# Twenty high parts of weight units made by ScalarE instead of GpSimd, around the two output projections of block 1 and the input of block 2's first layer

## The reference, cut to what matters

```python
x = layer_norm(DN_ALPHA * x + mix, ln1_g[layer], ln1_b[layer])
x = layer_norm(DN_ALPHA * x + sqrelu_mlp(x, mlp_w1[layer], mlp_w2[layer]), ln2_g[layer], ln2_b[layer])
...
def sqrelu_mlp(x, w1, w2):
    h = jax.nn.relu(x @ w1)
    return (h * h) @ w2
```

## Time and profile before

| | |
|---|---|
| median of 3 runs | 1706.57 us (1700.12 to 1709.83) |
| the profiled execution | 1702.99 us, its span 1701.1 us |
| mean granted clock of TensorE | 0.986 of full speed |
| TensorE matmuls, busy | 1610.1 us (95%) |
| VectorE, busy | 998.9 us (59%) |
| ScalarE, busy | 836.7 us (49%) |
| GpSimd, busy | 77.3 us (5%), 60 instructions |

### The profile page before, as it was taken

The page is one execution under the profiler, slowest core; times in us unless marked ns, Lnnn a source line. Parts: engine busy times, 40 slices in busy tenths (PEclk is TensorE's granted clock), DMA queues, the critical chain, the costliest instruction groups (busy, mean ns, idle before and its releaser), DMA issues.

```text
span 1701.1 us, 26801 instructions
## 1 busy us (share of the span) xinstructions
PE 1610.1 (95%) x10898; PEld 1407.7 (83%) x10898; DVE 998.9 (59%) x1521; ACT 836.7 (49%) x1479; POOL 77.3 (5%) x60
## 2 busy tenths in 40 slices
PE   7998999999999999999988999999999998889997
PEld 6887789998889999987546588888888885679997
DVE  6855865556686556679754553333333688565555
ACT  5434175554726566353474462424243455665554
POOL 1200300001030000000000100000000100000000
PEclk9999999999999999999999999999999999999999
DMA  8733665556756555533101532222322141135551
GB/s 311 266 111 125 256 228 178 184 185 221 272 174 224 179 184 183 196 137 108 41 1 50 200 116 93 87 99 97 100 87 99 63 148 38 62 124 176 185 185 49
DMA packets 69939, 247.53 MB, mean 146 GB/s; under 512 B 7504, under 2 KB 10576, under 8 KB 69712
## 3 DMA queue, kind: packets, MB, share of 16 engines
q1 hardware_dynamic: 69840, 246.18, 42.4%
HBM read 245.10 MB, written 1.05 MB: 145 GB/s over the span
## 4 chain that ended last, share of the span: by engine, by line
PE 74%; DVE 12%; issue 7%; ACT 5%; DMA 1%; POOL 0%; SPq 0%; DVEq 0%; ACTq 0%; POOLq 0%
PE psum L375 20%; PE psum L377 20%; PE psum L376 19%; PE psum L1122 2%; DVE lo_ring L336 2%; PE psum L390 1%; PE psum L391 1%; PE psum L392 1%; DVE c_soft L2160 1%; DMA raw_ring<-weights 1%; ACT c_p L1945 1%; DVE c_p L2168 1%; PE psum L1774 1%; PE psum L490 1%; PE psum L403 1%
## 5 line engine op out<-in xcount | busy, mean ns | idle before, releaser
L375 PE MATMUL psum<-x_hi,hi_ring 128*128 128x256 f32 (+1 forms) x1464 | 460.5, 315 | 11.6 <-DVE x_lo L881 10.1
L336 DVE TENSOR_TENSOR lo_ring<-raw_ring,hi_ring 128x1024 fp32r<-128x1024 f32 x348 | 432.6, 1244 | 60.9 <-PE psum L377 21.1
L377 PE MATMUL psum<-x_hi,lo_ring 128*128 128x256 f32 (+1 forms) x1464 | 455.9, 311 | 0.0
L376 PE MATMUL psum<-x_lo,hi_ring 128*128 128x256 f32 (+1 forms) x1464 | 455.8, 311 | 0.0
L348 ACT ACTIVATE hi_ring<-raw_ring 128x1024 fp32r<-128x1024 f32 x292 | 307.4, 1054 | 266.2 <-PE psum L377 248.3
L375 PEld LDWEIGHTS psum<-x_hi,hi_ring 128*128 128x128 f32 x1464 | 281.1, 192 | 33.5 <-issue 15.1
L375 PE MATMUL psum<-hid_hi,hi_ring 128*128 128x256 f32 (+1 forms) x992 | 303.4, 306 | 0.3 <-DVE lo_ring L336 0.3
L377 PE MATMUL psum<-hid_hi,lo_ring 128*128 128x256 f32 (+1 forms) x992 | 302.1, 305 | 0.0
L376 PE MATMUL psum<-hid_lo,hi_ring 128*128 128x256 f32 (+1 forms) x992 | 301.2, 304 | 0.0
L376 PEld LDWEIGHTS psum<-x_lo,hi_ring 128*128 128x128 f32 x1464 | 281.1, 192 | 15.0 <-issue 0.2
L377 PEld LDWEIGHTS psum<-x_hi,lo_ring 128*128 128x128 f32 x1464 | 280.9, 192 | 14.8
(11 more groups left out here) (424 smaller groups left out, 1996.8 us busy)
## 6 DMA issues: line engine op xcount, KB each, us to landing
raw_ring<-weights SPq DMA_DIRECT2D x460, 512.0 KB, 3.4
h_const<-hyb_consts SPq DMA_DIRECT2D x1, 1088.0 KB, 11.5
x<-xT SPq DMA_DIRECT2D x1, 1024.0 KB, 6.6
x<-ctxT SPq DMA_DIRECT2D x1, 1024.0 KB, 16.8
outT<-x SPq DMA_DIRECT2D x4, 256.0 KB, 2.5
shared<-shared_consts SPq DMA_DIRECT2D x1, 398.0 KB, 13.4
par<-params SPq DMA_DIRECT2D x1, 301.5 KB, 6.7
```

The lines of the kernel that those rows point to most:

```text
L336: nc.vector.tensor_tensor(lo_ring[:, s, :], raw_ring[:, UNIT_AT[u] % RAW_SLOTS, :], hi_ring[:, s, :].bitcast(F32), ALU.subtract).then_inc( ...
L375: nc.tensor.matmul(bank(u % BANKS, T), w_hi, hi[:, k, 0:T], start=(k == 0), stop=False)
L376: nc.tensor.matmul(bank(u % BANKS, T), w_hi, lo[:, k, 0:T], start=False, stop=False)
L377: last = nc.tensor.matmul(bank(u % BANKS, T), w_lo, hi[:, k, 0:T], start=False, stop=(k == KT - 1))
```

## The change

Three edits. A new list `ENTRY_HI` is added to `ACT_HI`: units 26 to 33 (the last four of the first output projection and the first four of the MLP), 118 to 125 (the same at the second), and 186 to 189 (the first of block 2). GpSimd's loop leaves them out, as it does with all of `ACT_HI`, and keeps 36 of 56. A new function `entry_hi_act` calls `next_hi_act` for the eight units of an output projection; it is called between the mixer's part of ScalarE's program and the squares of the norm, for both projections. In `mlp_act` the high parts are also made for the last four steps of the last quarter where m < 2; for m = 0 the units four ahead are 94 to 97, which are not in the list, so that nothing is issued, and for m = 1 they are 186 to 189.

```diff
--- before.py
+++ after.py
@@ -102,8 +102,9 @@
 SPLIT_UNITS = [u for u in range(UNITS) if u not in NATIVE]
 SPLIT = {u: n for n, u in enumerate(SPLIT_UNITS)}
 MLP_HI = [u for base in (U_MLP1, U_MLP2, *U_L2MLP) for u in range(base + SPLIT_SLOTS, base + MLP_UNITS)]
+ENTRY_HI = [u for base, ahead in ((U_MLP1, SPLIT_SLOTS), (U_MLP2, SPLIT_SLOTS), (U_L2, 0)) for u in range(base - ahead, base + SPLIT_SLOTS)]
 ACT_HI = sorted([*range(SPLIT_SLOTS, 14), *range(U_REC + SPLIT_SLOTS, U_REC + KT + SPLIT_SLOTS), *range(U_L2 + SPLIT_SLOTS, U_L2 + L2_IN + 3 + KT),
-                 *range(U_L2B + L1_NATIVE + SPLIT_SLOTS, U_L2B + L2_IN + 3 + KT), *MLP_HI])
+                 *range(U_L2B + L1_NATIVE + SPLIT_SLOTS, U_L2B + L2_IN + 3 + KT), *MLP_HI, *ENTRY_HI])
 LAST_SPLIT = len(SPLIT_UNITS)
 LATE = 4
 LATE_UNITS = [U_L2B - LATE + j for j in range(LATE)]
@@ -346,6 +347,11 @@
             act.wait_ge(raw_loaded[slot], 16 * (UNIT_AT[v] // RAW_SLOTS) + 16)
             wait_unit(act, u)
             nc.scalar.activation(hi_ring[:, SPLIT[v] % SPLIT_SLOTS, :], raw_ring[:, slot, :], ACT.Copy).then_inc(act_hi_ready, 1)
+
+    def entry_hi_act(act, base):
+
+        for u in range(base, base + KT):
+            next_hi_act(act, u)
 
     def next_lo(dve, u):
         ahead = SPLIT[u] + LEAD
@@ -1381,7 +1387,7 @@
                 nc.scalar.activation(relu2[:, j % 2, 0:T], relu[:, j % 2, 0:T], ACT.Square).then_inc(flag("hidden_hi"), 1)
                 next_hi_act(act, u)
             for j in range(KT):
-                if i < QUARTERS - 1 or j < KT - SPLIT_SLOTS:
+                if i < QUARTERS - 1 or j < KT - SPLIT_SLOTS or m < 2:
                     next_hi_act(act, base + 2 * KT * i + KT + j)
                 if m == 1 and i in (1, 2) and j % 2 == 0:
                     context_scaled_act(act, link, [4 * (i - 1) + j // 2])
@@ -2332,6 +2338,7 @@
         def _(act):
             link = Link(act, act_step)
             hyb_act(act, link)
+            entry_hi_act(act, U_HOUT)
             squares_act(act, 0, SEQ, y, "centered", 0, "mean0")
             norm_rstd_act(act, link, 0, SEQ, 0)
             layer_norm_act(act, 0, 0, "ln1_g", "ln1_b", "norm0")
@@ -2341,6 +2348,7 @@
             norm_rstd_act(act, link, 1, SEQ, 0)
             layer_norm_act(act, 1, 1, "ln2_g", "ln2_b", "norm1")
             rec_act(act, link, 1)
+            entry_hi_act(act, U_ROUT)
             squares_act(act, 2, SEQ, y, "centered", 2 * KT, "mean2")
             norm_rstd_act(act, link, 2, SEQ, 0)
             layer_norm_act(act, 3, 2, "ln1_g", "ln1_b", "norm2")
```

## The result

The changed kernel takes 1716.03 us at the median against 1704.96 us for the kernel before (20 runs each): the ratio is 1.0069, with an interval of 1.0056 to 1.0083, or +11.8 us (+9.5 to +14.2). One of the 20 executions of either kernel took far longer (2664.55 and 5036.93 us) and has no part in the ratio. The profiled execution of the changed kernel took 1724.45 us with a span of 1722.7 us, one of the slowest of its 20; that of before took 1702.99 us. So the two traces differ by more than the medians do, and each stage has to be read by itself.

The account below looks back on a forecast made before the run. TensorE was taken as the bound, busy 95% and 74% of the chain. Terms +4.45 + 4.40 + 3.56 - 0.83 - 0.15 = +11.43 us on the 1706.57 us median gave 1718.0 us, range 1710 to 1723 us.

Parts of the forecast that it names:

- The wait behind unit 33 and unit 125: At both output projections' norms, ScalarE waits for a raw tile ahead of the squares: +4.45 and +4.40 us.
- the lower bound of 3.6 us: First norm: low end of the tile's effect on the squares, given as 3.6 to 4.5 us.
- the landing of the tile: Raw tile of unit 33 loads only after unit 32's low part, landing at 218.79 us; unit 125's at 520.41 us.
- The clock: TensorE's longer gap before both square sums lowers its granted clock: 2 x 1.78 us, 3.56 us.
- The seven chances in ten for two falls: Chance given to TensorE's clock falling at both norms' square sums, +3.56 us together.
- The low level: Rival: low clock outlasts the square sum, 3.5 us at one or both places, +13.15 to +14.87 us; chance 0.10.
- The gains on VectorE: Both output projections: VectorE's work shortens with GpSimd idle, gaining 0.83 us at the first and 0.15 us at the second.
- the wait of 0.91 us: First output projection: TensorE's wait before the matmul at 198.27 us, expected to vanish, gain 0.83 us.
- The rule of the port: GpSimd and VectorE share a port pair, one waiting for the other; by it alone -1.0 us or somewhat better.
- Block 2's first units: Units 186 to 189 on ScalarE: cost and gain nothing, hidden by TensorE's context half of unit 186.
- No stage gives the delay back: Stages beyond the touched places should only shift; a later stage giving the delay back would make the prediction wrong.

Follow-up runs that it names:

- two units alone: Changed kernel with only units 33 and 125 on ScalarE ahead of the squares, the other eighteen high parts on GpSimd: 1719.81 us, ratio 1.0085.
- behind the squares: Changed kernel with the high parts of units 33 and 125 placed after the norm's squares in ScalarE's program, all twenty still on ScalarE: 1704.66 us, ratio 1.0005.
- tile loaded sooner: Changed kernel with the raw tiles of units 33 and 125 ahead of the seven modulation tiles in the load stream: 1708.26 us, ratio 1.0010.
- the second measurement: The changed kernel measured again with no edit: 1717.49 us, ratio 1.0081 to the kernel before.
- gap filled: Changed kernel with eighteen extra TensorE matmuls before the sum of the squares at both output projections: 1712.24 us, ratio 1.0056.
- one place only: Changed kernel with unit 125 back on GpSimd, so only unit 33 holds ScalarE ahead of the squares: 1708.56 us, ratio 1.0023.
- projections only: Changed kernel with units 33, 125 and 186 to 189 left to GpSimd; ScalarE makes 26 to 32 and 118 to 124: 1703.27 us, ratio 0.9979.
- block 2 only, first set: Changed kernel with only units 186 to 189 moved to ScalarE: 1706.88 us, ratio 1.0018 to the kernel before.
- block 2 only, second set: Same kernel with only units 186 to 189 moved to ScalarE, measured again on a different chip: 1702.36 us, ratio 0.9981.
- the second kernel with the gap filled: Changed kernel with the same eighteen extra TensorE matmuls at both output projections, measured again beside the changed kernel: 1713.10 us, ratio 1.0048.

## Why the prediction was right

The forecast was 1718.0 us, +11.4 us; measured were 1716.03 us and +11.8 us. Point by point:

- **The wait behind unit 33 and unit 125**, +4.45 and +4.40 us forecast: the mechanism is as told, shown by four kernels (two units alone have the loss; without them, behind the squares or with the tile loaded sooner it is gone). The size was over: 3.50 and 4.27 us in the profiled execution, 3.41 and 3.54 us in that of the second measurement; three of the four lie below the lower bound of 3.6 us. The term that was mis-sized is the landing of the tile. I took over the 4.2 us that passed before between the end of the low part of unit 32 and the start on GpSimd; in the changed kernel it was 3.3 us (214.90 to 218.21) and 4.1 us. Where VectorE was relieved, as here, it was 3.2 to 4.6 us at the fifteen places in eight traces in which an engine waited for this load, below 3.6 us at seven of them; where it was not, 4.2 to 4.9 us at all eight places in four traces. A likely reason is that the low part of unit 31 begins 2.95 us ahead of that of unit 32 (210.81 and 213.76), before only 1.51 us (211.87 and 213.38), which lets the modulation tile in front load sooner. It is not the whole reason: with the same 2.95 us the first place of the kernels with the gap filled took 4.0 and 4.6 us. What makes one load short and another long stays open.
- **The clock**, 2 x 1.78 us forecast: a fall at both places, with 1.69 and 2.94 us; the second is larger than the 1.78 us taken from one gap of the kernel before. In the four traces in which ScalarE held the squares and TensorE's gap was left open, the sum of the squares was slow at all seven places, between 5.41 and 6.66 us; in the traces with the gap filled or closed it took 3.72 to 3.75 us. The seven chances in ten for two falls were too careful for gaps of 4.1 to 5.3 us. The low level did not reach beyond the sum: the five modulation tiles behind it took 2.37 us at both places, as before. The rule of the Trainium skill (TensorE: Matmul & The Clock Gate, Part 1), that an idle array is put back to half rate, had both falls as certain; these seven gaps agree with it; the gap of 3.10 us without a fall shows that idle time on TensorE does not bring one every time.
- **The gains on VectorE**, -0.83 and -0.15 us forecast: the wait of 0.91 us is gone from TensorE's list, the instruction behind it shrank from 1.09 to 0.24 us, as forecast from one elsewhere (0.26 us). The rule of the port in the Trainium skill (SBUF — State Buffer, section "SBUF: two separate sides") agrees: all adds take 0.42 us. Its sum, a gain of 1 us, was not the whole effect. The size is shown by TensorE's rows: from the matmuls ahead of unit 22's first (line 471, now 477) to the modulation tiles of the mean it takes 19.43 us (195.12 to 214.55) in place of 20.28 us (193.88 to 214.16), and at the second place 1.51 us pass from the last matmul to the modulation tiles (521.11 to 522.62) in place of 1.67 us: gains of 0.85 and 0.16 us. In the ratios of the kernels without the wait it is too small to see (0.9996, 1.0005, 0.9979); with the granted clock taken into account it shows in two of the three (below).
- **Block 2's first units**, 0 forecast: shown by the rows of the stage, where the context half hides the earlier centring.
- **No stage gives the delay back**: so it was. The sum from the trace of the changed kernel is 12.40 - 1.01 = 11.4 us; that the forecast is also 11.4 us is in part luck, since delays that were too large (8.85 us against 7.77) made up for falls that were too small (3.56 us against 4.63). By the trace of the second measurement, with shorter delays and 1.69 us at both sums, the same sum is 9.3 us. A gain that was not forecast, 0.3 us, is in neither: TensorE's second wait for `x` in the first MLP is 0.77 us in place of 1.07 us.

The profiled execution of the changed kernel is 21.5 us longer than that of before, not 11.4 us. Its mean granted clock is 0.977 against 0.986, and most of that difference comes from stages that the change does not touch (see the section on the hardware).

## What to carry to other kernels

Before moving an operation to an idle engine, look at what stands behind it in that engine's program and at the last of its waits: an engine that does nothing else, as GpSimd here, can sit in a wait for a load at no cost, while on the engine that makes the squares the same wait costs its whole length. Idle time of an engine is cover only up to the next instruction that the chain needs; put the moved work behind that instruction, or have its data there in time. A delay of 4 us on the path of TensorE should be priced with the clock that it may lose, here 1.7 to 2.9 us more.

## What the runs showed of the hardware

**Falls of the clock differ between executions of the same program.** Over layer 1 of block 2, which no edit touched, the granted clock was 0.97 before, 0.93 in the first trace of the changed kernel and 0.97 in its second (windows of 120 us over the same stages, in this order):

```profile
1420.00:1540.00 120.00, 101.07 (x679) 83.60 (x678) 77.39 (x126) 73.05 (x149) 8.23 (x4) 0.97 0.25 80
1439.00:1559.00 120.00, 101.70 (x654) 83.20 (x653) 74.41 (x120) 71.98 (x148) 8.24 (x4) 0.93 0.24 75
1428.00:1548.00 120.00, 101.11 (x679) 83.50 (x678) 77.44 (x126) 73.00 (x149) 8.24 (x4) 0.97 0.25 79
```

TensorE's longest waits for the squares and for x there are of the same lengths in all three (3.0 and 3.1 us); what differs is how many low stretches follow such gaps.

**These falls make most of the spread of the times.** The record lists the mean granted clock of each execution. Over the 81 executions of the kernel before that have it, the clock lies between 0.979 and 0.989, and the time falls as it rises (correlation -0.89), by 1.3 us for each 0.001. Fitted within all kernels together it is 1.35 us. With that slope every kernel can be compared with the kernel before at the same clock (worked out afterwards from the record, with no expectation ahead of it; in brackets twice the standard error):

| kernel | executions | mean clock | difference of the means | at the same clock |
|---|---|---|---|---|
| before | 81 | 0.9851 | 0 | 0 |
| changed | 25 | 0.9816 | +11.9 us | +7.2 us (0.7) |
| gaps filled | 18 | 0.9844 | +8.4 us | +7.5 us (0.7) |
| 33 and 125 back on GpSimd | 12 | 0.9845 | -0.5 us | -1.3 us (0.9) |
| behind the squares | 12 | 0.9846 | +0.1 us | -0.5 us (0.9) |
| tile loaded sooner | 12 | 0.9840 | +2.0 us | +0.6 us (0.9) |
| only 33 and 125 | 5 | 0.9812 | +14.3 us | +9.1 us (1.3) |
| one place only | 12 | 0.9829 | +5.1 us | +2.2 us (0.9) |
| projections only | 12 | 0.9858 | -2.4 us | -1.3 us (0.9) |
| block 2 only, first set | 12 | 0.9836 | +2.4 us | +0.4 us (0.9) |
| block 2 only, second set | 12 | 0.9867 | -2.3 us | 0.0 us (0.9) |

Of the changed kernel's loss 4.7 us go with the clock, about what its longer sums say (4.63 and 3.38 us in the two traces), and 7.2 us are the late squares less the gains; with the gaps filled that part is the same. The gain of some 1 us shows in two of the three kernels without the wait, and the two sets of block 2 agree. Of the 21.5 us between the profiled pair, 0.009 of clock makes 12 us.

**The interval of one set of runs is not the whole uncertainty.** The same kernel gave 1.0018 (1.0001 to 1.0034) and 0.9981 (0.9965 to 0.9997) in two sets. In the ratio alone differences of 0.2% of this kernel stay open; the mean clock of the sets has to be looked at beside it.

**The time from a free slot to a loaded tile** (from the end of the low part ahead of it, at the start of the centring, to the high part) was 3.2 to 4.9 us for a tile of 512 KB at 23 places of twelve traces: 3.3 and 4.1 us at the two places of the changed kernel, 4.6 us at the first place of the second kernel with the gap filled, 4.9 us at the second place of the second set of block 2.
